# The latents' norm sums of six feature tiles, added up on GpSimd instead of multiplied on TensorE

## What is computed

```
def ffn_sublayer(x, shift, scale, gate, w_in, w_out, ln_g, ln_b):
    y = swiglu_2(modulate_2(x, shift, scale), w_in, w_out)
    return layer_norm(ALPHA * x + 0.5 * gate * y, ln_g, ln_b)

for i in range(DEPTH_2):                       # layer 0: gMLP mixer, layer 1: attention
    x_lat = ffn_sublayer(x_lat, ...)           # f0 / f2
    x_ctx = ffn_sublayer(x_ctx, ...)
    y_lat, y_ctx = mixer(modulate_2(x_lat, ...), modulate_2(x_ctx, ...))
    x_lat = layer_norm(ALPHA * x_lat + m_lat[5] * y_lat, ...)
    x_ctx = layer_norm(ALPHA * x_ctx + m_ctx[5] * y_ctx, ...)      # not in the last layer
    x_lat = ffn_sublayer(x_lat, ...)           # f1 / f3
    x_ctx = ffn_sublayer(x_ctx, ...)           # not in the last layer
return x_lat
```

## Time and profile before

| | us |
|---|---|
| median of three runs | 2569.93 |
| the three runs | 2569.39, 2569.93, 2573.72 |
| span of the profiled execution, from first to last instruction | 2571.0 |
| TensorE busy in it | 2465.7 |
| VectorE busy | 1849.9 |
| ScalarE busy | 1103.7 |
| GpSimd busy | 0.2 |

### The profile page before, as it was taken

The page is one execution under the profiler, slowest core; times in us unless marked ns, Lnnn a source line. Parts: engine busy times, 40 slices in busy tenths (PEclk is TensorE's granted clock), DMA queues, the critical chain, the costliest instruction groups (busy, mean ns, idle before and its releaser), DMA issues.

```text
span 2571.0 us, 39389 instructions
## 1 busy us (share of the span) xinstructions
PE 2465.7 (96%) x15574; PEld 2235.4 (87%) x15574; DVE 1849.9 (72%) x3597; ACT 1103.7 (43%) x1650; POOL 0.2 (0%) x4
## 2 busy tenths in 40 slices
PE   4999999989999999999999999999999999998998
PEld 3998989989989888788888998888998888877998
DVE  7888988878877745768787669896785444676655
ACT  3444565444453324724232652232642322645444
POOL 0000000000000000000000000000000000000000
PEclk8999999999999999999999999999999999999999
DMA  8886766758856531654444266676273333212663
GB/s 317 301 268 222 252 213 229 257 191 274 292 179 203 186 98 51 216 155 129 148 135 127 83 193 208 191 236 198 97 256 131 115 107 96 79 61 74 197 192 104
DMA packets 161384, 453.68 MB, mean 176 GB/s; under 512 B 17713, under 2 KB 21297, under 8 KB 161201
## 3 DMA queue, kind: packets, MB, share of 16 engines
q1 hardware_dynamic: 161200, 451.16, 54.1%
HBM read 450.04 MB, written 1.05 MB: 175 GB/s over the span
## 4 chain that ended last, share of the span: by engine, by line
PE 78%; DVE 5%; ACT 2%; issue 1%; DMA 1%; ACTq 0%; DVEq 0%; SPq 0%
PE PS L1182 25%; PE PS L1184 24%; PE PS L1183 24%; DVE own L1671 1%; PE PS L1209 1%; PE PS L1336 1%; PE PS L1207 1%; PE PS L1382 1%; DVE X L1652 0%; PE PS L1365 0%; ACT Uh L1462 0%; ACT own L1401 0%; DMA SCR<-in_ma 0%; ACT NT L1466 0%; PE PS L1310 0%
## 5 line engine op out<-in xcount | busy, mean ns | idle before, releaser
L1182 PE MATMUL PS<-Uh,own 128*128 128x256 f32 (+1 forms) x2064 | 655.3, 317 | 43.5 <-DVE Ul L1752 20.5
L1183 PE MATMUL PS<-Ul,own 128*128 128x256 f32 (+1 forms) x2064 | 644.6, 312 | 0.0
L1184 PE MATMUL PS<-Uh,own 128*128 128x256 f32 (+1 forms) x2064 | 644.3, 312 | 0.0
L1401 ACT ACTIVATE own<-raw 128x1024 fp32r<-128x1024 f32 x425 | 444.1, 1054 | 360.5 <-PE PS L1184 300.6
L1671 DVE TENSOR_TENSOR own<-raw,own 128x1024 fp32r<-128x1024 f32 x425 | 515.5, 1219 | 68.0 <-ACT own L1401 67.7
L1182 PEld LDWEIGHTS PS<-Uh,own 128*128 128x128 f32 x2064 | 399.5, 194 | 72.7 <-issue 36.5
L1183 PEld LDWEIGHTS PS<-Ul,own 128*128 128x128 f32 x2064 | 400.7, 194 | 19.9 <-issue 0.2
L1184 PEld LDWEIGHTS PS<-Uh,own 128*128 128x128 f32 x2064 | 400.3, 194 | 20.1
L1182 PE MATMUL PS<-Hh,own 128*128 128x256 f32 (+1 forms) x1096 | 348.5, 318 | 1.0 <-DVE own L1671 0.6
L1184 PE MATMUL PS<-Hh,own 128*128 128x256 f32 (+1 forms) x1096 | 343.9, 314 | 0.0
L1183 PE MATMUL PS<-Hl,own 128*128 128x256 f32 (+1 forms) x1096 | 343.9, 314 | 0.0
(11 more groups left out here) (222 smaller groups left out, 3875.4 us busy)
## 6 DMA issues: line engine op xcount, KB each, us to landing
MODS<-in_mm SPq DMA_DIRECT2D x168, 256.0 KB, 3.5
SCR<-in_mm SPq DMA_DIRECT2D x136, 256.0 KB, 3.8
raw<-in_f0i SPq DMA_DIRECT2D x64, 512.0 KB, 4.1
raw<-in_f1i SPq DMA_DIRECT2D x56, 512.0 KB, 3.6
raw<-in_f2i SPq DMA_DIRECT2D x56, 512.0 KB, 3.6
SCR<-in_ma SPq DMA_DIRECT2D x88, 256.0 KB, 5.1
raw<-in_w1i SPq DMA_DIRECT2D x44, 512.0 KB, 4.9
raw<-in_w2i SPq DMA_DIRECT2D x44, 512.0 KB, 4.5
```

The source lines that it names most:

```text
L1182: e.matmul(o, ll, rh, start=start, stop=False)
L1183: e.matmul(o, lh, rl, start=False, stop=False)
L1184: return e.matmul(o, lh, rh, start=False, stop=stop)
L1401: e.activation(parts(w.n)[0], raw[:, w.n % RING, :], ACT.Copy).then_inc(s["whi"].tell(w.n), 1)
```

## The change

In the four transitions the folds of the latents' norm are switched on, but made by GpSimd. `square` is called with the default `folded=FOLDED` and `pool=True`; the `fold` works carry `pool` and are skipped by VectorE; a new function for GpSimd walks the list and makes them, with a signal of its own, `pool_folded`. TensorE sums `NT` and tiles 6 and 7, and waits for `pool_folded` before the first. ScalarE's squares wait for `pool_folded` where they waited for TensorE's sums.

```diff
-    def square(self, t, k, folded=FOLDED):
+    def square(self, t, k, folded=FOLDED, pool=False):
+        t["pool"] = pool
...
         for i in range(j - n + 1, j + 1):
-            self.freed[i] = ("folded", (t["n"], k, "q"))
+            self.freed[i] = ("pool_folded" if t["pool"] else "folded", (t["n"], k, "q"))
...
-                self.square(self.tallies[q], mm, 0 if r is LAT and st in ("f0", "go", "f1", "f2") else FOLDED)
+                self.square(self.tallies[q], mm, pool=r is LAT and st in ("f0", "go", "f1", "f2"))
...
-                        on.wait_ge(s["folded"], (w.n, w.k, "q"))
+                        on.wait_ge(s["pool_folded" if w.pool else "folded"], (w.n, w.k, "q"))
...
-                elif w.what == "fold":
+                elif w.what == "fold" and not w.pool:
...
+        def gpsimd(e):
+            on = Queue(e)
+            nt_read = {"f0": ("nf", KT - 1), "f1": ("l01", KT - 1), "f2": ("l02", KT - 1)}
+
+            for w in plan.order:
+                lo, hi = w.r
+                if w.what == "fold" and w.pool:
+                    x, q = NT[:, lo // S, 0, :], NT[:, lo // S, 1, :]
+                    st = w.after[1][0]
+                    if w.k == 1:
+                        x0, q0 = X[:, 0, lo:hi], SQ[:, (w.j - 1) % 4, :]
+                        if st == "go":
+                            on.wait_ge(s["modded"], last_middle_mod)
+                        else:
+                            on.wait_ge(s["ulo"], nt_read[st])
+                    else:
+                        x0, q0 = x, q
+                        on.wait_ge(s["pool_folded"], (w.n, w.k - 1, "q"))
+                    on.wait_ge(s["acc"], w.after[1])
+                    e.tensor_tensor(x, x0, X[:, w.k, lo:hi], ALU.add).then_inc(s["pool_folded"].tell((w.n, w.k, "x")), 1)
+                    on.wait_ge(s["squared"], w.j)
+                    e.tensor_tensor(q, q0, SQ[:, w.j % 4, :], ALU.add).then_inc(s["pool_folded"].tell((w.n, w.k, "q")), 1)
+
         with nc.Block() as block:
+            block.gpsimd(gpsimd)
             block.tensor(tensor)
```

More of the change, by code:

```diff
@@ L136 @@
     eps: float = 0.0
+    pool: bool = False
 class Plan:
@@ L336, in fold @@
         for i in range(j - n + 1, j + 1):
-            self.freed[i] = ("folded", (t["n"], k, "q"))
-        self.put("fold", n=t["n"], k=k, r=t["r"], j=j, centred=t["centred"], after=t["before"](k))
+            self.freed[i] = ("pool_folded" if t["pool"] else "folded", (t["n"], k, "q"))
+        self.put("fold", n=t["n"], k=k, r=t["r"], j=j, centred=t["centred"], after=t["before"](k), pool=t["pool"])
         if last:
@@ L347, in sums @@
         self.put("sums", n=t["n"], k=k, r=t["r"], j=-1 if j is None else j, bank=t["bank"], centred=t["centred"],
-                 first=t["first"], final=k == KT - 1)
+                 first=t["first"], final=k == KT - 1, pool=t["pool"])
         t["first"] = False
@@ L971 @@
     "pooled", "roped1", "mapped", "y_lo", "masked", "weight1", "merged", "m_lo", "v_part", "v_stat", "v_normed", "mixed",
-    "sq_sum", "root_inv", "spreads", "head_x", "roped2", "weight2", "o_lo", "final_x")
+    "sq_sum", "root_inv", "spreads", "head_x", "roped2", "weight2", "o_lo", "final_x",
+    "pool_folded")
 def build(nc, T, out, plan, known):
```

## The result

The changed kernel takes 2577.2 us (median; 2574.6 to 2578.8), the kernel before, run beside it, 2573.2 us (2569.4 to 2576.7): 21 runs of each. The ratio is 1.0014, with a 95% interval of 1.0008 to 1.0020. So it is slower by about 4 us, clearly slower than before but within the 0.2% that I had called no change. The prediction said 2576.2, from 2560 to 2587; of its three outcomes it gave "slower" the largest chance, 0.40, and this one, "within", 0.31. The profiled execution took 2577.43 us with a span of 2575.3; the span of before is 2571.0, so the two profiles differ by 4.3 us, as the medians do, and can be compared step by step.

A forecast was written before the change was run, and what follows sets the result against it. TensorE, busy 2465.7 of 2571.0 us, was taken to bound the kernel. T1 +2.6, T2 +2.1, T3 +1.4 and T4 +0.2 sum to +6.3: 2577.3 by span, 2576.2 by median (1.1 lower); range 2560 to 2587.

The forecast's parts named there:

- TensorE loses five pairs and arrives earlier: Each transition: TensorE drops sums of tiles 0 to 4, reaching the folded pair 4.3 us sooner; 17.2 us over four.
- T3: Third transition, starting near 1814 us: forecast to end 1.4 us later.
- An add every 0.85 us: GpSimd's adds, start to start; eight remaining after tile 2's accumulation take 6.8 us.
- Holding: VectorE's two-input instructions and GpSimd's adds block each other: GpSimd's chain grows to 10.2 us, VectorE loses 2.6 per transition.
- The clock: After TensorE's 4.5 us wait for the folded sum, half clock for 5 us, costing 2.5 us in each transition.
- T1: First transition, starting near 1004 us: forecast to end 2.6 us later.
- T2: Second transition, behind `go`, starting near 1435 us: forecast 2.1 us later, including half a weight's low part.
- T4: Fourth transition, starting near 2189 us: forecast 0.2 us later, including half a weight's low part.
- What is covered: ScalarE's squares get GpSimd-freed buffers on time, two to three tiles behind; VectorE's and ScalarE's instruction lists don't change.
- No holding: Rival over the transitions: neither engine holds the other and no clock falls; sum -9.4, 2560.5 us; chance 0.30.
- Holding without the clock: Rival over the transitions: engines hold each other but the clock stays; sum +1.8, 2571.7 us; chance 0.14.
- All of the gain: Rival over the transitions: all 17.2 us of saved TensorE sums arrive, 2552.7 us; chance 0.04.

The follow-up runs named there:

- experiment 1: Changed kernel, but TensorE sums all eight latent tiles again while GpSimd still makes its 40 adds, their sums unused: 2577.7 us, ratio 1.0015 to before.
- experiment 2: Changed kernel with each of GpSimd's 40 adds replaced by a 128x512 memset and TensorE summing all eight tiles: 2573.5 us, ratio 0.9998 to before.
- experiment 4: Changed kernel plus ten matmuls with unused results on TensorE in front of each transition's folded sum: 2575.2 us, ratio 1.0009 to before.
- experiments 7: Changed kernel with only two tiles folded by GpSimd, two adds in each transition: 2574.3 us, ratio 1.0003 to before.
- experiment 11: Changed kernel with four tiles folded by GpSimd in T1, T3 and T4 and nothing in T2: 2573.2 us, ratio 0.9999 to before.
- experiment 8: Changed kernel with GpSimd making only the five adds of values per transition, TensorE summing all squares itself: 2580.0 us, ratio 1.0031 to before.
- experiment 9: Changed kernel with GpSimd folding six tiles in T2 alone, the other transitions as before: 2580.3 us, ratio 1.0023 to before.
- 10: Changed kernel with GpSimd folding six tiles in T1, T3 and T4, not in T2: 2576.5 us, ratio 1.0011 to before.
- experiment 3: Changed kernel with TensorE's folded pair of sums put behind the first context products instead of in front: 2580.1 us, ratio 1.0028 to before.
- 12: Kernel of experiment 9 plus sixteen matmuls with unused results in front of T2's folded sum: 2575.7 us, ratio 1.0008 to before.
- experiment 5: Changed kernel with the same folds made by VectorE instead of GpSimd in the four transitions: 2578.9 us, ratio 1.0025 to before.

## Why the prediction was right, step by step

The time was right (2577.2 us measured, 2576.2 predicted), and so were the direction and the mechanism. The outcome with the largest chance, slower by over 0.2%, did not come: it is slower by 0.14%. Two sizes were off, and two errors made the number better than the working.

1. *TensorE loses five pairs and arrives earlier*: right. It stood in front of the folded sum in all four transitions, in T3 4.1 us sooner than before (1829.92, less the 3.94 us by which the whole transition starts later, against 1830.08), where I had 4.3. The time saved is worth nothing, as experiment 1 shows.
2. *An add every 0.85 us*: 0.70 measured, where nothing is beside it (0.74 long), against the bounds of 0.42 and 1.74. The Trainium skill, "GPSIMD Engine Reference", section "Performance versus the Vector engine", has a ratio from which I had estimated 0.82; the rows decide for less.
3. *Holding*: right, and shown by experiments 1 and 2. VectorE lost 1.7 to 2.3 us a transition (2.6 forecast), though not as six equal holds of 0.43: a low part grows by up to 0.54, a norm by 0.15 at most, and `CF<-CF,M`, a seventh instruction with two SBUF inputs that I had overlooked, by 0.56. The fold was ready 8.8 us behind tile 2's accumulation in T3 (1823.62 + 0.39 to 1832.80), not 10.2: that is eight adds at 0.74 us (5.9), 1.7 us of being held and 1.2 us of standing still for the accumulations of tiles 3 and 5 and at the start, where I had 6.8, 2.7 and 0.7.
4. *The clock*: forecast as 2.5 us in every transition, behind a wait of 4.5 us. The waits were 2.4 to 4.3 us. The half clock lasted 3.4 us in T1, 10.2 in T2, none in T3 and 6.8 in T4. This is the term that was mis-sized: 10 us of the forecast's working, of which some 3 reached the end, 1.6 in T2 and 1.4 in T4. In T1 it cost nothing (experiment 4 has the same -0.2 at full clock), in T3 it did not come.
5. *What is covered*: the squares never waited for a buffer of GpSimd's, as forecast. What I left out is that ScalarE passes on VectorE's hold-up: in T2 the square of a tile that VectorE adds late (it waits 0.76 us for it) stands ahead of a weight's high part, and VectorE waits 0.70 us for that.
6. *The transitions*: T2 came out near for partly other reasons (+2.5 measured, 3.3 with what lies behind it, +2.1 forecast): the fold's readiness did not set its end, VectorE's chain did with 1.6 us, and the clock added the remainder. T1 (+2.6 forecast, -0.2 measured) and T3 (+1.4, -0.7) fall by the earlier fold and the milder clock. T4 is +1.4 instead of +0.2, all from the clock: with TensorE kept busy it is +0.1 (experiment 4).

The sum of +6.3 us was too large; +3.8 in the transitions with what lies behind T2, and +4.0 by the medians. What brought the forecast to within 1 us of the result is luck with the start: I set the span of 2571.0 against a median of 2569.9 and took off 1.1 us. More runs put before's median at 2573.2, and an execution's time lies 2.1 us above its span (2577.43 against 2575.3). A base 3.3 us too low hid a sum 2.3 us too high.

**The rivals.** *No holding* (2560.5) is refuted by the lengthened rows and by experiment 1. Its mark was that a transition's adds hold VectorE by less than 1 us; experiments 7 and 11 go that way (0 and 1.2 us), and reach before's time but no less, so the ending on the other side did not come even then. *Holding without the clock* (a sum of +1.8 us) is not what happened, but experiment 4 comes near to its condition: with the clock at 1.00 in three of four transitions it lies 1.8 us above before. *All of the gain* (2552.7) never came near.

**Open.** How the loss splits between the hold-up and the clock is known inside the transitions of single executions: over T2 1.6 and 1.6 us, over T4 about 0 and 1.4. Over many executions it is only known that the clock is lower in all of them, since the same waits are followed by half the clock in one and not in another. The size of experiment 8 stays unexplained, and so does the sum of 9 and 10 but for the waits for DMAs. The clock falls in experiment 1 too, where TensorE waits for nothing but low parts: hold-up and clock are not independent costs, and no run has the hold-up in T2 with a clock of 1.00.

## What to carry to other kernels

An engine that does nothing is not free to use while another reads the same memory: before moving elementwise work to GpSimd, look at what VectorE runs in just those microseconds, and count its instructions with two SBUF inputs, not the adds. What is taken off the engine with the largest busy share is worth its time only where that engine is the last to be waited for; here 17 us became waits, and these cost clock on top. Where a wait can't be removed, look at which chain it belongs to before putting other work into it: work that hangs on the same chain (experiment 3) only spreads the wait, while work that hangs on nothing (experiments 4 and 12) did no harm here.

## What the runs showed of the hardware

- GpSimd's fp32 add of 128x256 in SBUF: 0.74 us, a next one 0.70 us behind it; VectorE's takes 0.42 (0.34 from start to start, experiment 5). A memset of 128x512 on GpSimd: 0.53 us (experiment 2).
- The hold-up is not shared out but falls on the later one: 0.42 to 0.94 us for a low part, 0.17 to 0.72 us for an instruction of 8 columns, 0.74 to 1.26 us for an add. Memsets, which only write, hold nobody (experiment 2, 17 cases).
- The granted clock fell to half behind waits of 2.44 and 2.73 us, not behind one of 2.88 us, and in two executions (T4 of experiment 9, T2 of experiment 11) behind one of 1.53 us that had left it at 1.00 in others. 3.4 us at half clock cost 1.3 us where nothing else had changed (experiment 11, T2).
